# Attention K/V prefix projections moved between the steps of the gated linear attention stage

## The chip, the cores and the metric

The kernel runs on all eight cores of one Trainium2 chip, the same program on each. The time is the device time of the slowest core in microseconds. Nothing is exchanged between the cores. PE is TensorE (PEld its weight loads), DVE VectorE, ACT ScalarE, POOL GpSimd, SP SyncE.

## The reference, cut to what matters

One layer of a decoder for two groups of requests: two new prompts of 4096 tokens, and 32 sequences that each get 4 new tokens.

```
h = rmsnorm(x);  proj = h @ w_in        # gq gk gv gg glr | aq ak av
log_a = log_sigmoid(glr @ w_gk_up + b_gk) / 16
gla:  S_t = diag(a_t) S_{t-1} + k_t^T v_t ;  o_t = q_t S_t        (4 heads, 128 x 256 state)
att:  each query sees keys t - j*dil, j = 0..128, for dil 1, 4, 16  (8 heads of 128)
x = x + concat(rmsnorm(gla_o) * silu(gg), rmsnorm(att_o)) @ w_out
y = rmsnorm(x + square(relu(rmsnorm(x) @ w_up)) @ w_down)
```

D_MODEL is 2048. A core owns 1024 prompt tokens and the 16 new tokens of four sequences. To have the GLA state and the keys of up to 2048 earlier tokens, it computes these for the tokens before its own as well.

## The kernel before

A core goes through its prompt in four groups of 1024 tokens, `for g in range(4)`; group 3 holds its own tokens, groups 0 to 2 the prefix. For each group:

1. **Norm** (`ssq_norm`). SP and POOL by turns load 16 chunks of x into four buffers; ACT squares, DVE scales into `hT`, PE sums the squares with a matrix of ones, and DVE and POOL multiply by the inverse root. `hT` is bf16, 16 chunks of 128 features.
2. **GLA** (`gla_group`, L648). PE projects the low-rank gate, then K and V of head 0. Then for each of the 4 heads 14 steps are issued (in a prefix group): A1 for each half of 512 tokens (gate matmuls, then ACT), A2 for each half (cumulated gate, ACT, DVE at L587, POOL's multiply at L589), A3 for each half (transposes, ACT), and 8 state steps B, one for 128 tokens. B is a PE matmul, then DVE's update of the state `Sf` (L641), then POOL's cast to `Sb` (L644). Behind each step comes one item of the next head's projections (`proj_items`, L659): 2 K items of 16 matmuls 128x512, then 8 V tiles of 16 matmuls 128x256. Head 3 has no next head, and its steps follow one another bare.
3. **K/V prefix** (`kv_prefix_group`, L781), in groups 1 and 2 only, between two barriers. For each of the 8 attention heads, K and V are projected for the group's 1024 tokens: 4 items of 16 matmuls 128x512, each copied by ACT to a staging buffer of `kvst`, and stored by SP to a scratch tensor in HBM, which attention reads much later.

After group 3 come the K/V outputs, the attention heads, the attention of the 16 new tokens, w_out, and the MLP; none of this changes.

**Order and waits.** Each engine executes its own instructions in program order. `P.op` collects for each operation the operations it depends on, through trackers (`Trk`) of what last wrote a tile and what has read it since. `emit` turns each dependency into a wait instruction of its own (L110), unless the engine has already waited for that value or a later one of the same semaphore. So an operation that overwrites a tile issues one wait for each of the matmuls that read it, except those that an earlier wait covers. A barrier makes every engine wait for the last operation of each engine and the last transfer of every DMA slot.

**Weights.** `w_in` lies in HBM in fp32 (`wflat`) and is cast to bf16 by the DMA, which POOL issues (L290). `wload` (L403) has the list of all loads in order, and when load i is asked for it has issued load i + 1 as well; the blocks go round in three buffers (`wblk`):

```python
while len(wstate["issued"]) <= min(i + 1, len(WLIST) - 1):
    wstate["issued"].append(_wissue(WLIST[len(wstate["issued"])]))
```

A prefix head's block (128 columns of K, 128 of V) and a GLA head's V block are 1024 KB as written, a K block 512 KB. All matmuls are recorded at line 319 (transposes at 322), ACT's at 325. `AT` is a buffer of 16 chunks for the results of both attentions; groups 0 to 2 don't use it. `sqb` are two buffers of the norm stage, 1040 columns each.

Of the kernel before, what the change touches and what calls it, by code (L numbers as in the profile page):

```python
# [190 lines left out]
WLIST = None  # L191
# [32 lines left out]
def _build(nc, P):  # L224
# [64 lines left out]
    def dma(q, out, in_, reads=(), writes=()):  # L289
        return P.op(q, lambda e: e.dma_start(out=out, in_=in_), reads=reads, writes=writes, dma=True)  # L290
# [36 lines left out]
    class Rot:  # L327
        def __init__(self, arena, shape, dt, n):
            self.b = [arena.alloc(shape, dt) for _ in range(n)]
            self.t = [Trk() for _ in range(n)]  # L330
            self.i = 0

        def get(self):
            k = self.i % len(self.b)
            self.i += 1
            return self.b[k], self.t[k]
# [66 lines left out]
    def wload(col_specs, src=None, rows=None):  # L403
        i = wstate["i"]
        wstate["i"] += 1
        if WLIST is None:
            WLOG.append(col_specs)
            return _wissue(col_specs)
        assert WLIST[i] == col_specs
        while len(wstate["issued"]) <= min(i + 1, len(WLIST) - 1):  # L410
            wstate["issued"].append(_wissue(WLIST[len(wstate["issued"])]))
        return wstate["issued"][i]

    def proj_fm(wb, wt, wc, m, parts, evac):
        for (c0, n) in parts:
            ps, pt = ps_f()
            for kc in range(16):
                mm(ps[0:m, 0:n], wb[:, kc, wc:wc + m], hT[:, kc, c0:c0 + n], kc == 0, kc == 15,
                   reads=[wt, hT_t[kc]], writes=[pt])
            evac(ps, pt, c0, n)  # L420
# [224 lines left out]
            return stageB  # L645
        return [A1, A2, A3], [mk(i) for i in range(4)]

    def gla_group(g, own):  # L648
        parts = PARTS_OWN if own else PARTS_PRE
        N = NTOK if own else 1024  # L650
        P.op("pool", lambda e: e.memset(glrT[:, 0:N], 1.0), writes=[glrT_t])
        wb, wt = wload([(0, C_GLR, 16)])

        def ev_glr(ps, pt, c0, n):
            act(glrT[0:16, c0:c0 + n], ps[0:16, 0:n], AF.Copy, reads=[pt], writes=[glrT_t])
        proj_fm(wb, wt, 0, 16, parts, ev_glr)
        ntile = 9 if own else 8

        def proj_items(h, G):  # L659
            gkT, gkT_t, gqT, gqT_t, gv, gv_t, ggs, ggs_t = (G["gkT"], G["gkT_t"], G["gqT"], G["gqT_t"], G["gv"], G["gv_t"],  # L660
                                                            G["ggs"], G["ggs_t"])
            cols = [(0, C_GK + h * 128, 128)] + ([(128, C_GQ + h * 128, 128)] if own else [])
            wb, wt = wload(cols)

            def ev_k(ps, pt, c0, n):
                act(gkT[:, c0:c0 + n], ps[:, 0:n], AF.Copy, reads=[pt], writes=[gkT_t])

            def ev_q(ps, pt, c0, n):
                P.op("dve", lambda e: e.tensor_copy(out=gqT[:, c0:c0 + n], in_=ps[:, 0:n]), reads=[pt], writes=[gqT_t])
            for p_ in parts:  # L670
                proj_fm(wb, wt, 0, 128, [p_], ev_k)
                yield
            if own:
                for p_ in parts:
                    proj_fm(wb, wt, 128, 128, [p_], ev_q)
                    yield
            wb, wt = wload([(0, C_GV + h * 256, 256)])
            for ti in range(ntile):
                m = 128 if ti < 8 else 16

                def ev_v(ps, pt, ti=ti, m=m):
                    P.op("dve", lambda e: e.tensor_copy(out=gv[0:m, ti, :], in_=ps[0:m, 0:256]), reads=[pt], writes=[gv_t[ti]])  # L682
                proj_tm(wb, wt, 256, ti * 128, m, ev_v)
                yield
            if own:
                wb, wt = wload([(0, C_GG + h * 256, 256)])
                for vh in range(2):
                    def ev_g(ps, pt, c0, n, vh=vh):
                        act(ggs[:, vh, c0:c0 + n], ps[:, 0:n], AF.Silu, reads=[pt], writes=[ggs_t])
                    for p_ in parts:  # L690
                        proj_fm(wb, wt, vh * 128, 128, [p_], ev_g)
                        yield

        def head_norm(h, G):
            ggs, ggs_t = G["ggs"], G["ggs_t"]
            pss = [ps_f() for _ in parts]
            for vh in range(2):
                q, qt = sqb.get()
                act(q[:, 0:N], o_h[:, vh, 0:N], AF.Square, reads=[o_t], writes=[qt])
                for (c0, n), (ps, pt) in zip(parts, pss):  # L700
                    mm(ps[:, 0:n], onesb[:], q[:, c0:c0 + n], vh == 0, vh == 1, reads=[qt, ct], writes=[pt])
            for (c0, n), (ps, pt) in zip(parts, pss):
                act(sgate[:, c0:c0 + n], ps[:, 0:n], AF.Ln, reads=[pt, ct], writes=[sgate_t], scale=1.0 / 256,
                    bias=epsb[:, 0:1])
            act(sgate[:, 0:N], sgate[:, 0:N], AF.Exp, reads=[sgate_t], writes=[sgate_t], scale=-0.5)
            for vh in range(2):
                P.op("dve", lambda e, vh=vh: e.scalar_tensor_tensor(
                    out=o_h[:, vh, 0:N], in0=o_h[:, vh, 0:N], scalar=nw[:, NW_GLA + vh:NW_GLA + vh + 1],
                    in1=sgate[:, 0:N], op0=ALU.mult, op1=ALU.mult), reads=[o_t, sgate_t, ct], writes=[o_t])
                P.op("pool", lambda e, vh=vh: e.tensor_mul(out=AT[:, 2 * h + vh, 0:N], in0=o_h[:, vh, 0:N],  # L710
                                                          in1=ggs[:, vh, 0:N]),
                     reads=[o_t, ggs_t], writes=[AT_t[2 * h + vh]])

        for _ in proj_items(0, GB[0]):
            pass
        for h in range(4):
            G = GB[h % 2]
            nxt = proj_items(h + 1, GB[(h + 1) % 2]) if h < 3 else None
            (a0, b0), (a1, b1) = gla_batch(h, 0, own, G), gla_batch(h, 1, own, G)
            steps = [a0[0], a1[0], a0[1], a1[1], a0[2], a1[2]] + b0 + b1  # L720
            if own:
                steps.append(lambda h=h, G=G: gla_tile(h, 1024, 16, own, True, G))
                steps.append(lambda h=h, G=G: head_norm(h, G))
            nit = (24 if own else 10)
            per = -(-nit // len(steps))
            for st in steps:
                st()
                if nxt is not None:
                    for _ in range(per):
                        if next(nxt, "done") == "done":  # L730
                            nxt = None
                            break
            if nxt is not None:
                for _ in nxt:
                    pass

    A3 = Arena(nc, A1_mark)
    ks_s = A3.alloc([16, 1024], F32)
# [39 lines left out]
    atts_b = A3.alloc([16, 1024], BF16)  # L778
    atts_bt = Trk()

    def kv_prefix_group(g):  # L781
        for h in range(8):
            wb, wt = wload([(0, C_AK + h * 128, 128), (128, C_AV + h * 128, 128)])
            for which in range(2):
                st_, stt = kvst.get()

                def ev(ps, pt, c0, n, st_=st_, stt=stt):
                    act(st_[:, c0:c0 + n], ps[:, 0:n], AF.Copy, reads=[pt], writes=[stt])
                proj_fm(wb, wt, which * 128, 128, PARTS_PRE, ev)
                dma("sp", kvscr[which, h, :, (g - 1) * 1024:g * 1024], st_[:], reads=[stt], writes=[kvscr_t[which][h]])  # L790

    def kv_outputs():
        for which, (cb, outd, outs, sdst, sdt) in enumerate(((C_AK, k_o, ks_o, ks_s, ks_t), (C_AV, v_o, vs_o, vs_s, vs_t))):
# [216 lines left out]
    for g in range(4):  # L1010
        own = g == 3
        if DEBUG == "gla0" and not own:
            continue
        parts = PARTS_OWN if own else PARTS_PRE

        def src_chunks(kc, g=g, own=own):
            b, t = xc.get()
            dma("sp" if kc % 2 == 0 else "pool", b[:, 0:1024], xTv[kc, :, g * 1024:(g + 1) * 1024], writes=[t])
            if own:
                P.op("pool", lambda e, b=b, kc=kc: e.tensor_copy(out=b[:, 1024:1040], in_=xs_all[:, kc, :]), reads=[xs_t], writes=[t])  # L1020
            return b[:, 0:(NTOK if own else 1024)], [t]
        ssq_norm(src_chunks, parts, NW_ATTN, hT, hT_t, 2048.0)
        dumpf(0, rB[:, :], [rB_t])
        dumpb(0, hT[:, 0, :], [hT_t[0]])
        dumpb(1, hT[:, 15, :], [hT_t[15]])
        gla_group(g, own)
        if g in (1, 2):
            P.barrier()
            kv_prefix_group(g)
            P.barrier()  # L1030
    for h in range(4):
        dma("sp", gst_o[h], Sf[:, h, :], reads=[Sf_t[h]])
    P.barrier()
# [256 lines left out]
```

How the kernel before makes its waits and increments, by code:

```python
            def run(ename, eng):  # L98
                waited = {}
                for o in ops:
                    if o.eng != ename:
                        continue
                    for d in sorted(o.deps):
                        do = ops[d]
                        if do.dma:
                            sem, key = dsem[do.eng][do.slot], ("d", do.eng, do.slot)
                        else:
                            sem, key = csem[do.eng], ("c", do.eng)
                        if waited.get(key, 0) < do.val:
                            eng.wait_ge(sem, do.val)
                            waited[key] = do.val
                    if o.fn is None:
                        continue
                    ins = o.fn(eng)
                    if o.dma:
                        ins.then_inc(dsem[ename][o.slot], 16)
                    elif o.inc:
                        ins.then_inc(csem[ename], 1)
```

## Time and profile before

| | |
|---|---|
| median of the runs shown | 3796.25 us (3791.42 and 3801.07) |
| the profiled execution | 3794.15 us, span of its slowest core 3792.6 us |
| spans of the eight cores | 3767.1 to 3792.6 us |
| mean granted TensorE clock | 0.80 to 0.81 on every core |
| PE busy | 2777.2 us (73%) |
| DVE, ACT, POOL busy | 1197.2, 818.6, 813.4 us |
| chain that ended last | PE 63%, DMA 15%, issue 6%, ACT 6%, DVE 6%, POOL 4% |
| norm, group 1 | about 232 to 306 us |
| GLA, group 1 | 306.3 to 445.2 us |
| K/V prefix, group 1 | 445.2 to 557.4 us |
| norm, GLA, prefix of group 2 | to 630, 769 and 881.5 us |
| MLP | 2712 to 3690 us |

Times are from the first instruction of the slowest core, core 1. "Granted clock" is the share of full speed that TensorE was given: 1.00 is 2.4 GHz, 0.50 is 1.2 GHz. A timeline row is a run of like instructions: its start, the time from the first to the last, the engine and line, what it writes and reads, the count, and in brackets how long the engine was idle before it and what ended that. Waits and DMA issues themselves are not counted as busy time.

### The profile page before, as it was taken

The page shows a single profiled execution, that of the slowest core. Times are in us where ns is not written, and L with a number is a line of the kernel's source. Part 1 is how long each engine was busy: PE and PEld are TensorE (multiplying, and loading weights), DVE is VectorE, ACT ScalarE, POOL GpSimd, SP SyncE. Part 2 cuts the span into 40 slices and gives each one's busy share as a digit, 9 for nine tenths or more (in the row PEclk, how much of TensorE's full clock was granted, in tenths as well). Part 3 has the DMA queues.
Part 4 walks back from the last instruction along what each step waited for, and adds up shares of the span by engine and source line. Part 5 has one row for each costly group of instructions (what it writes and reads, how often), then busy time and mean ns, then how long its engine had stood idle before and what let it go on. Part 6 is the DMA issues. An engine that isn't in the chain of part 4 may idle for free.

```text
span 3792.6 us, 65066 instructions; the slowest of 8 cores (3767.1 to 3792.6 us)
## 1 busy us (share of the span) xinstructions
PE 2777.2 (73%) x17044; PEld 1474.5 (39%) x17044; DVE 1197.2 (32%) x2009; ACT 818.6 (22%) x2051; POOL 813.4 (21%) x1293
## 2 busy tenths in 40 slices
PE   2857886894888588767777222358499999999995
PEld 0635533641454375333333100023144444444443
DVE  3232203202222202333334433341343434243434
ACT  2131112112123212443344222220200010101003
POOL 3122103201221202222223233420311121211110
PEclk9968897996888598666666555568799999999998
DMA  4232343253332243112110144454234334342422
GB/s 116 45 90 51 70 106 98 45 109 109 57 63 50 67 111 74 29 40 45 29 29 18 17 70 69 72 106 112 45 57 79 66 69 76 59 87 49 90 46 91
DMA packets 76667, 257.02 MB, mean 68 GB/s; under 512 B 11609, under 2 KB 25433, under 8 KB 64898
## 3 DMA queue, kind: packets, MB, share of 16 engines
q0 software_dynamic: 43136, 186.93, 26.6%
q1 hardware_dynamic: 33170, 65.92, 5.0%
q8 instruction: 148, 2.42, 0.2%
q14 instruction: 213, 1.74, 0.1%
HBM read 394.89 MB, written 28.05 MB: 112 GB/s over the span
## 4 chain that ended last, share of the span: by engine, by line
PE 63%; DMA 15%; issue 6%; ACT 6%; DVE 6%; POOL 4%; ACTq 0%; POOLq 0%; DVEq 0%; SPq 0%
PE psf L319 60%; ACT sb L325 6%; DMA sb<-wflat 4%; DMA sb<-xT 3%; PE psb L322 3%; DMA sb<-ck 2%; DMA sb<-cv 2%; DVE sb L376 2%; POOL sb L376 1%; DMA sb<-wo_flat 1%; DVE sb L933 1%; DVE sb L929 1%; POOL sb L1110 1%; DVE sb L641 1%; DVE sb L1144 0%
## 5 line engine op out<-in xcount | busy, mean ns | idle before, releaser
L319 PE MATMUL psf<-sb,sb 128*128 128x512 bf16 (+8 forms) x16316 | 2717.3, 318 | 933.5 <-ACT sb L325 342.0
L319 PEld LDWEIGHTS psf<-sb,sb 128*128 128x128 bf16 (+3 forms) x16316 | 1413.0, 105 | 2179.9 <-issue 1262.6
L325 ACT ACTIVATE sb<-psf 128x512 f32<-128x512 f32 (+7 forms) x585 | 264.2, 465 | 1956.9 <-PE psf L319 1792.0
L1118 DVE TENSOR_TENSOR sb<-sb,psf 128x512 f32<-128x512 f32 (+1 forms) x768 | 380.9, 516 | 624.4 <-PE psf L319 613.1
L325 ACT ACTIVATE sb<-sb 128x1024 bf16<-128x1024 f32 (+7 forms) x273 | 185.4, 696 | 571.2 <-DVE sb L936 239.3
L857 DVE TENSOR_TENSOR sb<-sb,psf 128x128 f32<-128x128 f32 (+2 forms) x424 | 217.3, 512 | 264.3 <-PE psf L319 194.1
L848 POOL TENSOR_TENSOR sb<-sb,sb 128x64 bf16<-128x64 f32 (+3 forms) x424 | 164.6, 402 | 407.8 <-ACT sb L325 404.9
L1110 POOL TENSOR_TENSOR sb<-sb 128x512 bf16<-128x512 f32 (+1 forms) x192 | 146.5, 763 | 459.0 <-ACT sb L325 445.6
L325 ACT ACTIVATE sb<-psb 64x128 bf16<-64x128 bf16 (+4 forms) x488 | 140.4, 296 | 282.7 <-PE psb L322 249.3
L322 PE MATMUL psb<-sb,sb 128*128 128x128 bf16 (+3 forms) x584 | 155.4, 301 | 48.2 <-POOL sb L589 30.2
L366 DVE TENSOR_SCALAR sb<-sb,sb 128x1024 bf16<-128x1024 f32 (+1 forms) x80 | 57.6, 757 | 358.0 <-DMA sb<-xT 200.2
L325 ACT ACTIVATE sb<-psf,sb 128x64 f32<-128x64 f32 (+5 forms) x463 | 148.6, 370 | 9.7 <-PE psf L319 7.2
L682 DVE CAST sb<-psf 128x256 bf16<-128x256 f32 x132 | 56.0, 424 | 263.1 <-PE psf L319 243.3
L376 POOL TENSOR_TENSOR sb<-sb,sb 128x1024 bf16<-128x1024 bf16 (+1 forms) x40 | 124.1, 3134 | 68.8 <-ACT sb L325 68.8
L290 POOL DMA_DIRECT2D sb<-wflat x80 | 44.6, 559 | 396.6 <-PE psf L319 372.8
L929 DVE TENSOR_TENSOR sb<-sb,psf 128x512 f32<-128x512 bf16 x96 | 65.8, 685 | 199.6 <-PE psf L319 164.0
L376 DVE TENSOR_TENSOR sb<-sb,sb 128x1024 bf16<-128x1024 bf16 (+1 forms) x40 | 114.3, 2927 | 24.9 <-ACT sb L325 24.9
L322 PEld LDWEIGHTS psb<-sb,sb 128*128 128x128 bf16 (+3 forms) x584 | 78.6, 141 | 96.2 <-issue 70.3
L644 POOL CAST sb<-sb 128x256 bf16<-128x256 f32 x128 | 51.6, 403 | 237.6 <-DVE sb L641 181.4
L820 DVE CAST sb<-psf 128x512 bf16<-128x512 f32 (+1 forms) x24 | 12.5, 519 | 284.6 <-PE psf L319 284.5
L641 DVE SCALAR_TENSOR_TENSOR sb<-sb,sb,psf 128x256 f32<-128x256 f32 x128 | 61.0, 477 | 105.1 <-PE psf L319 87.6
L325 ACT ACTIVATE sb<-sb,sb 128x128 bf16<-128x128 bf16 (+1 forms) x194 | 78.9, 407 | 26.8 <-DMA sb<-v_s 6.4
(63 smaller groups left out, 597.0 us busy)
## 6 DMA issues: line engine op xcount, KB each, us to landing
sb<-wflat POOLq DMA_DIRECT2D x56, 1024.0 KB, 9.2
sb<-wu_flat POOLq DMA_DIRECT2D x16, 2048.0 KB, 15.4
sb<-w_down POOLq DMA_DIRECT2D x16, 2048.0 KB, 13.9
sb<-xT SPq DMA_DIRECT2D x48, 512.0 KB, 5.4
sb<-xT POOLq DMA_DIRECT2D x32, 512.0 KB, 6.0
sb<-wflat POOLq DMA_DIRECT2D x20, 512.0 KB, 5.0
kvscr<-sb SPq DMA_DIRECT2D x32, 256.0 KB, 3.1
sb<-kvscr SPq DMA_DIRECT2D x16, 512.0 KB, 5.0
```

The costliest lines, as they stand in the source:

```text
L319: P.op("pe", lambda e: e.matmul(out, lhsT=lhsT, rhs=rhs, start=start, stop=stop), reads=reads, writes=writes)
L322: P.op("pe", lambda e: e.transpose(out, in_, ident), reads=reads, writes=writes)
L325: P.op("act", lambda e: e.activation(out=out, in_=in_, func=func, **kw), reads=reads, writes=writes)
L366: P.op("dve", lambda e, kc=kc, s_ap=s_ap: e.tensor_scalar_mul(out=dst[:, kc, 0:N], in0=s_ap, scalar1=nw[:, nw_col + kc:nw_col + kc + 1]), ...
L376: P.op(eng, lambda e, kc=kc: e.tensor_mul(out=dst[:, kc, 0:N], in0=dst[:, kc, 0:N], in1=rB[:, 0:N]), reads=[dst_t[kc], rB_t], writes=[dst_ ...
L641: P.op("dve", lambda e: e.scalar_tensor_tensor(out=Sf[:, h, :], in0=Sf[:, h, :], scalar=bl[:, i:i + 1], in1=psS[:, 0:256], op0=ALU.mult, o ...
L682: P.op("dve", lambda e: e.tensor_copy(out=gv[0:m, ti, :], in_=ps[0:m, 0:256]), reads=[pt], writes=[gv_t[ti]])
L848: P.op("pool", lambda e, p_=p_, e_=e_, nk=nk, nq=nq, mbase=mbase: e.tensor_mul(out=p_[0:nk, 0:nq], in0=e_[0:nk, 0:nq], in1=amask[0:nk, mba ...
L857: P.op("dve", lambda e, ps2=ps2, qsl=qsl, nq=nq: e.tensor_add(out=acc[:, :, qsl], in0=acc[:, :, qsl], in1=ps2[:, 0:512].rearrange("p (a b) ...
L929: P.op("dve", lambda e, pr=pr, Kb=Kb, hh=hh: e.tensor_mul(out=pr[:, hh * 512:(hh + 1) * 512], in0=Kb[:, hh * 512:(hh + 1) * 512], in1=psQ[ ...
L1110: P.op("pool", lambda e, hb=hb, r_=r_, fc=fc, c0=c0, n=n: e.tensor_mul(out=hb[:, fc, c0:c0 + n], in0=r_[:, 0:n], in1=r_[:, 0:n]), reads=[r ...
L1118: P.op("dve", lambda e, ps=ps, dc=dc, c0=c0, n=n: e.tensor_add(out=x1T[:, dc, c0:c0 + n], in0=x1T[:, dc, c0:c0 + n], in1=ps[:, 0:n]), read ...
```

## The change

The prefix projections become a generator, `kv_prefix_items(g)`, which yields after each item of 16 matmuls, 32 items in all. `gla_group` takes it as `extra` and draws one item after each step, behind the item of the next head's projections; what is left at the end is drawn then. The two barriers around the prefix stage are gone. The weights no longer come through `wload`: the generator issues the load of a head's block itself, from POOL, into one half of the chunks 0 to 7 of `AT`, by turns, and goes on with that head's first item. The outputs are staged in the two buffers of `sqb`.

```diff
--- before.py
+++ after.py
@@ -645,7 +645,7 @@
             return stageB
         return [A1, A2, A3], [mk(i) for i in range(4)]
 
-    def gla_group(g, own):
+    def gla_group(g, own, extra=None):
         parts = PARTS_OWN if own else PARTS_PRE
         N = NTOK if own else 1024
         P.op("pool", lambda e: e.memset(glrT[:, 0:N], 1.0), writes=[glrT_t])
@@ -730,9 +730,14 @@
                         if next(nxt, "done") == "done":
                             nxt = None
                             break
+                if extra is not None and next(extra, "done") == "done":
+                    extra = None
             if nxt is not None:
                 for _ in nxt:
                     pass
+        if extra is not None:
+            for _ in extra:
+                pass
 
     A3 = Arena(nc, A1_mark)
     ks_s = A3.alloc([16, 1024], F32)
@@ -778,16 +783,40 @@
     atts_b = A3.alloc([16, 1024], BF16)
     atts_bt = Trk()
 
-    def kv_prefix_group(g):
+    class _Alias:
+        def __init__(self, rot):
+            self.rot, self.i = rot, 0
+
+        def get(self):
+            k = self.i % len(self.rot.b)
+            self.i += 1
+            return self.rot.b[k], self.rot.t[k]
+    kvst2 = _Alias(sqb)
+
+    def kv_prefix_items(g):
         for h in range(8):
-            wb, wt = wload([(0, C_AK + h * 128, 128), (128, C_AV + h * 128, 128)])
+            kvw_flat = AT[:, 4 * (h % 2):4 * (h % 2) + 4, :].rearrange("p a b -> p (a b)")[:, 0:4096]
+            kvw_t = AT_t[4 * (h % 2):4 * (h % 2) + 4]
+            key = ((C_AK + h * 128, 128), (C_AV + h * 128, 128))
+            if WLIST is None:
+                WOFF.setdefault(key, None)
+                dma("pool", kvw_flat[:, 0:16], wflat[:, 0:16], writes=kvw_t)
+            else:
+                dma("pool", kvw_flat, wflat[:, WOFF[key]:WOFF[key] + 4096], writes=kvw_t)
+            wb = kvw_flat.rearrange("p (kc n) -> p kc n", kc=16)
             for which in range(2):
-                st_, stt = kvst.get()
+                st_, stt = kvst2.get()
 
                 def ev(ps, pt, c0, n, st_=st_, stt=stt):
                     act(st_[:, c0:c0 + n], ps[:, 0:n], AF.Copy, reads=[pt], writes=[stt])
-                proj_fm(wb, wt, which * 128, 128, PARTS_PRE, ev)
-                dma("sp", kvscr[which, h, :, (g - 1) * 1024:g * 1024], st_[:], reads=[stt], writes=[kvscr_t[which][h]])
+                for (c0, n) in PARTS_PRE:
+                    ps, pt = ps_f()
+                    for kc in range(16):
+                        mm(ps[:, 0:n], wb[:, kc, which * 128:(which + 1) * 128], hT[:, kc, c0:c0 + n], kc == 0, kc == 15,
+                           reads=list(kvw_t) + [hT_t[kc]], writes=[pt])
+                    ev(ps, pt, c0, n)
+                    yield
+                dma("sp", kvscr[which, h, :, (g - 1) * 1024:g * 1024], st_[:, 0:1024], reads=[stt], writes=[kvscr_t[which][h]])
 
     def kv_outputs():
         for which, (cb, outd, outs, sdst, sdt) in enumerate(((C_AK, k_o, ks_o, ks_s, ks_t), (C_AV, v_o, vs_o, vs_s, vs_t))):
@@ -1023,11 +1052,7 @@
         dumpf(0, rB[:, :], [rB_t])
         dumpb(0, hT[:, 0, :], [hT_t[0]])
         dumpb(1, hT[:, 15, :], [hT_t[15]])
-        gla_group(g, own)
-        if g in (1, 2):
-            P.barrier()
-            kv_prefix_group(g)
-            P.barrier()
+        gla_group(g, own, kv_prefix_items(g) if g in (1, 2) else None)
     for h in range(4):
         dma("sp", gst_o[h], Sf[:, h, :], reads=[Sf_t[h]])
     P.barrier()
```

## Rows read from the trace of the kernel before

**Rows 1.** Busy time by stretch; its first line names the columns

```profile
core 1: us, PE busy (x) PEld busy (x) DVE busy (x) ACT busy (x) POOL busy (x), PEclk, DMA share, GB/s
...
306.30:445.20 138.90, 113.64 (x833) 86.45 (x833) 33.43 (x72) 24.61 (x48) 24.56 (x46) 0.90 0.25 49
...
445.20:557.40 112.20, 112.19 (x512) 50.35 (x512) 0.00 (x0) 18.54 (x31) 4.29 (x8) 0.99 0.48 102
...
425.00:445.00 20.00, 9.02 (x54) 6.93 (x51) 7.80 (x15) 4.87 (x10) 6.82 (x14) 0.66 0.00 1
...
445.20:448.30 3.10, 3.10 (x8) 1.14 (x9) 0.00 (x0) 0.00 (x0) 1.12 (x2) 0.50 0.00 0
...
448.30:455.00 6.70, 6.70 (x33) 3.01 (x31) 0.00 (x0) 1.20 (x2) 0.00 (x0) 1.00 0.87 147
```

**Rows 2.** PE's waits, GLA stage, then prefix stage: total us, times, longest

```profile
PE psf L319 <- DMA sb<-wflat: 10.8, 3, 4.2
...
PE psb L322 <- POOL sb L589: 8.4, 3, 5.7
...
PE psf L319 <- POOL sb L644: 7.3, 1, 7.3
```

**Rows 3.** The chain of waits that ended last: start us, us, what

```profile
238.99 5.02 DMA sb<-xT
...
299.30 6.87 DMA sb<-wflat
...
368.01 7.37 DMA sb<-wflat
...
400.13 7.58 DMA sb<-wflat
...
445.20 112.21 PE psf L319 x512
...
558.17 2.03 DMA kvscr<-sb
...
560.76 6.63 DMA sb<-xT
...
623.05 6.86 DMA sb<-wflat
```

**Rows 4.** Timeline, first GLA stage, up to the first A1 steps

```profile
313.92 0.53 POOL L290 DMA_DIRECT2D sb<-wflat  x1 [8.96 <-PE psf L319]
...
327.28 4.22 PEld L319 LDWEIGHTS psf<-sb,sb 17*128 17x128 f32 x24 [0.21 <-issue]
...
331.92 9.71 PEld L319 LDWEIGHTS psf<-sb,sb 17*128 17x128 f32 x72 [0.42 <-issue]
```

**Rows 5.** Timeline of heads 0 to 2 in the same stage

```profile
337.62 0.67 ACT L325 ACTIVATE sb<-psf 128x512 f32<-128x512 f32 x2 [0.29 <-PE psf L319]
...
339.17 1.03 POOL L589 TENSOR_TENSOR sb<-sb,sb 128x512 bf16<-128x512 f32 x1 [24.72 <-DVE sb L587]
...
347.74 0.59 POOL L290 DMA_DIRECT2D sb<-wflat  x1 [7.53 <-issue]
...
349.55 0.58 PE L322 MATMUL psb<-sb,sb 128*128 128x128 bf16 x4 [5.66 <-POOL sb L589]
...
364.64 0.48 DVE L641 SCALAR_TENSOR_TENSOR sb<-sb,sb,psf 128x256 f32<-128x256 f32 x1 [0.70 <-PE psf L319]
...
365.25 0.40 POOL L644 CAST sb<-sb 128x256 bf16<-128x256 f32 x1 [0.78 <-DVE sb L641]
...
368.01 0.59 POOL L290 DMA_DIRECT2D sb<-wflat  x1 [2.35 <-PE psf L319]
...
381.76 1.91 PE L319 MATMUL psf<-sb,sb 128*128 128x256 bf16 x16
```

**Rows 6.** POOL's queue, wait instructions of line 110 in 340 to 348 us

```profile
L110 POOLq EVENT_SEMAPHORE  x117: 17/17/17, 340.0 to 347.8; - x117
```

**Rows 7.** DMA issues in 440 to 560 us: count, KB each, median us to landing

```profile
sb<-wflat POOLq DMA_DIRECT2D x7, 1024.0 KB, 9.8
```

## The prediction

> **What bounds the kernel now.** I read the stages first, then what the matmul engine waits for in them, then the weight loads' place on the chain of waits and on POOL's stream. Groups 1 and 2 of the prompt each run one GLA stage and one K/V prefix stage; the second group repeats the first, so I work on group 1 and count twice. Its GLA stage is 138.9 us with PE busy for 113.6; the prefix stage is 112.2 us with PE busy for 112.2 [rows 1]. So only the GLA stage has holes: about 25 us. Of these, 5.7 is a wait for POOL and 4.2 twice a wait for a weight load (the third of the three, 2.4, is head 0's and stays) [rows 2]; 11 lie in the last 20 us, the fourth head, which has no projections to put between its steps [rows 1]. The prefix stage is sheer matmul work, 3.5 us for each of 32 items of 16 matmuls [rows 1, 3]. Its loads take 9.8 us [rows 7] and cost nothing, since each is asked for a whole head (14 us) ahead.
>
> **What changes, part by part.** (1) The 32 prefix items are put one behind each of the first 32 of 56 GLA steps, that is in heads 0 and 1 and four steps of head 2. PE's work is the same. The fourth head, with the 11 us of holes, gets none: no gain there. (2) The prefix weights no longer come through the prefetching loader. The generator asks POOL for head j's block and then emits, in the same turn, the first matmuls that read it. There are two buffers, but nothing is asked for early. Load j sits at step 4j, behind all that POOL has to do up to there. (3) The barriers go.
>
> Price of a load. Alone in flight in a GLA stage, a block of this size takes 7.4 to 7.6 us from issue to landing [rows 3]; in the prefix stage, with other traffic, the median is 9.8 [rows 7]. I take 7.5, since the new ones are mostly alone, and keep 9.8 for the range. The Trainium skill, "DMA: Bandwidth & Descriptors", section on the anatomy of a software-queue DMA, gives 2.0 us plus the bytes at 436 GB/s, so 4.4 us for 1 MiB; by that each stall below would be 3.1 us shorter and the sum +72 us instead of +115. The rows measured this very transfer, so they decide.
>
> Price of the waits ahead of it. Before a load may overwrite a buffer, POOL executes one wait for every matmul that read it: 117 are recorded in the 7.5 us hole before one issue [rows 5, 6], and a buffer with 32 readers has a hole of 2.35 us [rows 5]. That is 60 to 73 ns a wait. A prefix block has 64 readers: 3.8 to 4.7 us, I take 4.1. It is due where block j-2 was read after POOL's last wait, in both groups from j=2 on.
>
> Price of what gates POOL. In a state step (B) PE's matmul releases DVE's 0.48 us and that POOL's cast; with hand-overs the cast starts 0.75 us after the matmul, and the waits begin with it [rows 5]. In an A2 step ACT, DVE and POOL take 2.7 us from the matmul to the end of POOL's multiply [rows 5].
>
> Now each load j, timed from the matmul that gates it; PE's own work before it needs the block is a V tile of 1.9 us [rows 5], a K item of 3.5, a prefix item of 3.5, the gate matmuls of an A1 or A2 step 1.1 (two A1 steps start 4.6 us apart with a K item between [rows 4]), transposes 0.6.
> - j=0, step 0: nothing gates it but the load before it, issued at 313.9; PE comes to it only after the first A1 (327.3) and a K item, at 332 [rows 4]. Two loads of 7.5 in a row land by 329: no stall.
> - j=1, step 4: from the first A2 matmul POOL has 2.7, then a load with 128 waits (7.5), the second multiply (1.1), so the issue is at 12.0 and the landing at 19.5, up to 21.5 as the other transfer is still under way. PE arrives at 14.4. Stall 5.1 to 7.1, taken 6.1.
> - j=2 and j=5, B steps with a V tile: 0.75 + 4.1 + 7.5 - 1.9 = 10.4 each.
> - j=3 and j=6, B steps at which the projections of the next head have run out, so nothing lies between: 12.3 each.
> - j=4, A2 step: POOL's multiply starts at 1.7, then a K load with some 32 waits, then this one with some 48: issue at 6.8, landing 14.3 to 16.4, PE there at 1.9. Stall 12.3 to 14.5, taken 13.
> - j=7, step 28: issue at 5.2 behind another load, landing 12.7 to 16.2; PE has 3.5 + 1.1 + 3.5 to do. Stall 4.6 to 8.1, taken 6.3.
> Sum 70.8 us a group.
>
> What goes: the three stalls of 5.7, 4.2 and 4.2 [rows 2], since those loads and multiplies now have two items more of PE's work, or one of the new stalls, in front: -14.1.
>
> The clock: PE's granted clock is 0.50, the 1.2 GHz level, in the 3.1 us after PE restarts from a hole of 7 us, and 1.00 behind it [rows 1]. Each restart so loses 1.6 us of matmul work. Seven new ones, three fewer old ones: +6.2. The prefix items, which now run dense at the full level, are the ones that pay.
>
> The barrier behind the prefix stage: its last matmul ends at 557.4; the barrier drains the last store, and the first x load of POOL goes out at 560.8 [rows 3], the next group's weight load at 623.1, 65.7 us in all. Between groups 0 and 1, where there is no barrier, it is 60.3 us from that x load (239.0) to the weight load (299.3) [rows 3]: -5.3. It includes two x chunks that SP then loads early. The barrier ahead of the prefix stage makes PE wait 7.3 us for the last cast [rows 2], but without it the next norm stage stands behind the same chain of DVE and POOL: 0, between -7.3 and 0.
>
> Edits at nothing: the store of an item from two staging buffers instead of three (a store lands in 2.0 us [rows 3], a buffer comes round after two times two steps); 32 more copies on ACT, which is mostly idle in the stage [rows 1]. Were they all on the path, +19 us a group (0.6 each), which the range needn't hold.
>
> Sum for a group: 70.8 - 14.1 + 6.2 - 5.3 = +57.6 us, for both +115. The profiled execution took 3794.2 us (span 3792.6), 2.1 below the median of the runs shown; 3796.3 + 115 = **3911 us**, slower by 3.0%.
>
> **Bounds.** Low: shortest waits and loads (66 of stalls), the whole 7.3 of the first barrier back: +46 a group, 3888. With the loads at 9.8 us: +16 a group and the upper ends of j=1, 4, 7 (+4): 3952.
>
> **Rivals.**
> A, not slower: POOL gets to the loads early. The mechanism is j=0's: where no operation of POOL hangs on a recent matmul, the issue runs ahead of PE. If that held at all eight, the change would give -14.1 - 4.7 - 5.3 = -24.1 a group, 3748 us. The point that decides: the average stall, its restart at half clock included, must stay under 3.4 us (24.1 over 7). For it: the load at 313.9 is issued 18 us before use [rows 4]. Against it: at four of seven places the operation just before is the cast of the same step, and a 1 MB load never lands under 7.4 us; the ordinary loads, asked for a step or two ahead, still stall PE by 4.2 us [rows 2]. Chance 0.05; even this ends within 2%. Partly hidden stalls (about half, 3800 to 3870): 0.09.
> B, longer loads: seven of eight take the 9.8 us of the prefix stage, because of stores and other loads in flight: 3944. For it: [rows 7]; against: in the GLA stage only two loads per head compete. Chance 0.18.
> C, the interleaving pays more than I see, through the barriers and the fourth head: all holes of PE gone gives at most 25 + 7 a group, 3732 us. Against it: the items run out at step 32. Chance 0.02.
> D, the ACT and DVE chains are late behind the prefix copies: up to +19 a group on top, 3949. It needs ACT behind PE, while ACT is busy for 24.6 of 138.9 us [rows 1]. Chance 0.04.
> The forecast itself: 0.62.
>
> **Numbers.** About 2% (76 us, so 3872) is what a measurement can tell from no change. Slower: the forecast, B, D and a little of the partly hidden case, 0.86. Same: A and most of the partly hidden, 0.12. Faster 0.02. Range: 3862 to 3962.
>
> **What would show it.** In the changed kernel's trace PE should wait seven times in each of the two groups for the prefix weights' load, 5 to 14 us each, about 71 us in sum; on POOL some 64 waits should stand before each such issue; the three old stalls of the stage should be gone; the granted clock should drop after each hole; the stage from the first K item to the last cast should last some 314 us instead of 139 + 112; the fourth head should still take 20 us. Wrong would be: few or short waits for that load (A), or loads of 10 us (B). If PE's new waits are on ACT or DVE, D.

## The result, and the profile after

The changed kernel takes **3933 us** (median of 12 runs) against 3799 us for the kernel before (10 runs beside them): ratio **1.036**, 95% interval 1.034 to 1.039, slower by 134 us. Forecast were 3911 us and a range of 3862 to 3962. Some executions of every kernel, the one before too, fall into a slower condition of the chip that hits one die; ratios here come from undisturbed runs alone, and a time in microseconds behind a ratio is that ratio times 3799 where the median is disturbed.

The profiled execution's slowest core is core 0, with a span of 3927.8 us. First, where the time went. These are lines of the chain of waits of the changed kernel (start, us, what): the weight load that ends the norm stage of groups 2 and 3 (group 1's, at 301.66, stands among POOL's rows below).

```profile
698.19 6.58 DMA sb<-wflat
...
1102.51 10.14 DMA sb<-wflat
```

And the same one of the kernel before for group 3; those of groups 1 and 2 stand in [rows 3].

```profile
966.45 9.92 DMA sb<-wflat
```

Timeline rows of POOL after: the issue of group 1's weight load, the last cast of its GLA stage, the first x load of the next norm stage, and the last cast of group 2.

```profile
301.66 1.14 POOL L290 DMA_DIRECT2D sb<-wflat  x2
...
636.90 0.79 POOL L644 CAST sb<-sb 128x256 bf16<-128x256 f32 x1 [0.78 <-DVE sb L641]
637.64 1.12 POOL L290 DMA_DIRECT2D sb<-xT  x2
...
1029.65 0.40 POOL L644 CAST sb<-sb 128x256 bf16<-128x256 f32 x1 [0.78 <-DVE sb L641]
```

From the weight load of one group to that of the next it was 323.8 and 343.4 us (299.3, 623.05, 966.45) and is now 396.5 and 404.3 us (301.7, 698.2, 1102.5): +72.8 and +60.9, together 133.7 of the 134 us. These are the two slowest cores, core 1 before and core 0 after; the medians of all eight cores agree (324.2 and 341.8 us before, 395.6 and 405.6 after, together +135.2). So outside groups 1 and 2 next to nothing moved. Within them, GLA and prefix took 258.1 and 258.5 us before (299.3 to 557.4, 623.05 to 881.5) and take 336.0 and 331.9 now, up to the last cast: +77.9 and +73.4. From there to the next weight load it took 65.7 and 85.0 us and takes 60.6 and 72.5: -5.1 and -12.5.

What PE waits for in the interleaved stage of group 1, from the waits view (total us, times, longest); the rows that answer to [rows 2]:

```profile
PE psf L319 <- DMA sb<-wflat: 84.5, 7, 14.8
PE psb L322 <- POOL sb L589: 3.0, 2, 1.6
```

Seven waits for a weight load (310 to 640 us, so without head 0's own), where there were two in the run of the steps, and the one for POOL's multiply is gone. In group 2 they are seven again, 82.2 us. The timeline of PE shows each of the seven; the idle time before the row and what ended it stand in brackets.

```profile
369.20 5.93 PE L319 MATMUL psf<-sb,sb 128*128 128x512 bf16 x16 [9.33 <-DMA sb<-wflat]
...
404.53 17.88 PE L319 MATMUL psf<-sb,sb 128*128 128x512 bf16 x83 [11.50 <-DMA sb<-wflat]
436.21 27.06 PE L319 MATMUL psf<-sb,sb 128*128 128x512 bf16 x134 [13.80 <-DMA sb<-wflat]
478.03 12.21 PE L319 MATMUL psf<-sb,sb 128*128 128x512 bf16 x55 [14.75 <-DMA sb<-wflat]
...
514.45 21.03 PE L319 MATMUL psf<-sb,sb 128*128 128x512 bf16 x114 [11.51 <-DMA sb<-wflat]
549.45 21.58 PE L319 MATMUL psf<-sb,sb 128*128 128x512 bf16 x89 [13.97 <-DMA sb<-wflat]
580.70 26.27 PE L319 MATMUL psf<-sb,sb 128*128 128x512 bf16 x134 [9.66 <-DMA sb<-wflat]
```

All seven rows begin with a 128x512 matmul, a prefix item; they are j=1 to 7, and j=0 has no stall. Now POOL, ahead of the second of them: its issue rows in the timeline, the wait instructions in 390 to 397 us, and the loads in the chain with issue and time to landing.

```profile
396.69 0.53 POOL L290 DMA_DIRECT2D sb<-wflat  x1 [4.29 <-issue]
...
427.53 0.53 POOL L290 DMA_DIRECT2D sb<-wflat  x1 [4.00 <-issue]
```

```profile
L110 POOLq EVENT_SEMAPHORE  x67: 17/17/17, 391.9 to 396.7; - x67
```

```profile
358.42 10.64 DMA sb<-wflat
396.69 7.70 DMA sb<-wflat
427.53 8.16 DMA sb<-wflat
469.43 8.46 DMA sb<-wflat
506.61 7.70 DMA sb<-wflat
540.61 8.71 DMA sb<-wflat
568.85 11.71 DMA sb<-wflat
```

For 4.8 us POOL does nothing but get through 67 waits (the profile names no operation that it waited for), and only then does it issue a load that takes 7.7 us. And the clock, in two stretches (columns as in [rows 1]) behind the first stall, and over the stage:

```profile
308.70:642.90 334.20, 232.26 (x1325) 135.66 (x1344) 35.31 (x74) 44.13 (x82) 30.14 (x56) 0.84 0.29 63
...
369.20:372.30 3.10, 3.10 (x8) 1.14 (x9) 0.00 (x0) 0.00 (x0) 0.00 (x0) 0.50 0.00 0
372.30:376.00 3.70, 3.70 (x22) 1.92 (x20) 0.00 (x0) 0.78 (x2) 0.00 (x0) 0.78 0.00 0
```

In the first 3.1 us the granted clock is 0.50, the 1.2 GHz level, and eight matmuls of 512 columns get through instead of the fourteen of the dense stage before (512 in 112.2 us, at 0.99).

### The profile page after: what moved, and what is told of

It is laid out like the page before. It is cut to its first block, busy times and chain, and to the rows that moved or that the text cites. A ratio compares the mean times of both kernels' runs of the same rounds, so it can differ in the third digit from the quotient of the medians.

```text
span 3927.8 us, 64107 instructions; the slowest of 8 cores (3906.4 to 3927.8 us)
## 1 busy us (share of the span) xinstructions
PE 2771.7 (71%) x16816; PEld 1474.6 (38%) x17044; DVE 1196.8 (30%) x2009; ACT 815.1 (21%) x2051; POOL 814.5 (21%) x1293
## 4 chain that ended last, share of the span: by engine, by line
PE 60%; DMA 17%; issue 7%; DVE 6%; ACT 6%; POOL 4%; POOLq 0%; ACTq 0%; DVEq 0%; another core or an unknown queue 0%; SPq 0%
PE psf L319 58%; DMA sb<-wflat 6%; ACT sb L325 5%; DMA sb<-xT 3%; DMA sb<-ck 3%; PE psb L322 2%; DMA sb<-cv 2%; DVE sb L376 2%; POOL sb L376 1%; DMA sb<-wo_flat 1%; DVE sb L962 1%; POOL sb L1135 1%; DVE sb L641 1%; DVE sb L1143 1%; POOLq L110 0%
## 5 line engine op out<-in xcount | busy, mean ns | idle before, releaser
L319 PE MATMUL psf<-sb,sb 128*128 128x512 bf16 (+12 forms) x16088 | 2711.4, 318 | 1088.6 <-ACT sb L325 338.9
L319 PEld LDWEIGHTS psf<-sb,sb 128*128 128x128 bf16 (+4 forms) x16316 | 1412.9, 105 | 2326.5 <-issue 1429.4
L325 ACT ACTIVATE sb<-psf 128x512 f32<-128x512 f32 (+8 forms) x585 | 263.6, 464 | 2115.5 <-PE psf L319 1877.6
L849 DVE CAST sb<-psf 128x512 bf16<-128x512 f32 (+1 forms) x24 | 12.5, 520 | 283.7 <-PE psf L319 283.5
L589 POOL TENSOR_TENSOR sb<-sb,sb 128x512 bf16<-128x512 f32 x32 | 36.2, 1130 | 300.9 <-DVE sb L587 298.3
L587 DVE TENSOR_TENSOR sb<-sb,sb 128x512 f32<-128x512 f32 x32 | 23.7, 740 | 241.8 <-ACT sb L325 238.7
## 6 DMA issues: line engine op xcount, KB each, us to landing
sb<-wu_flat POOLq DMA_DIRECT2D x16, 2048.0 KB, 13.7
```

Source lines behind the costliest of these rows:

```text
L319: P.op("pe", lambda e: e.matmul(out, lhsT=lhsT, rhs=rhs, start=start, stop=stop), reads=reads, writes=writes)
L325: P.op("act", lambda e: e.activation(out=out, in_=in_, func=func, **kw), reads=reads, writes=writes)
```

## The experiments

Two theories were set against each other. **L**: the loss is the prefix loads, each asked for at its first use, with 64 waits ahead of it. **I**: cutting the dense prefix stage up costs by itself (copies, clock, order). Ratios are to the kernel before, with 95% intervals.

**e1_prefetch: the loads one head ahead.**

```diff
+        blocks = [load(0)]
         for h in range(8):
-            (load of head h, as in the change)
+            if h < 7:
+                blocks.append(load(h + 1))
+            wb, kvw_t = blocks[h]
```

> The changed kernel, but the prefix weights are asked for one head ahead: the blocks of heads 0 and 1 at the first step, and that of head h + 1 when head h's items begin, into the same two buffers. Theory L (the loss is late loads): PE's waits for the prefix weights, 84 us in group 1 of the changed kernel, go to under 5 us a group, and what is left is the gain that the prediction gave its rival A, 14.1 + 4.7 + 5.3 = 24 us a group: 3751 us, ratio to the kernel before 0.987. Theory I (the interleaving itself costs: copies on ACT, the dense stage cut up, the clock): the waits go but the time stays above the kernel before, 3810 to 3870. Theory Q (POOL's queue has no room, so even an early load is issued late): stalls of 5 us and more stay at most of the heads, above 3850.

Measured: 0.984 (0.983 to 0.986), about 3740 us. PE's waits in 299 to 720 us, which hold all of group 1's steps and the norm stage behind them:

```profile
PE psf L319 <- DMA sb<-wflat: 2.1, 2, 1.1
```

The 84.5 us of waits have become 2.1, and the kernel is 5% faster than the changed one, 1.6% faster than the one before. Theory I and the expectation's Q (POOL's queue has no room for an early load) fall: everything else of the change is still in, and it pays. From one group's first K item to the next one's it is 296.8 and 316.9 us on core 1 against 323.7 and 346.5 before: -27 and -29.5 a group, where the prediction's rival A had put -24.1.

**e2_onewait: no string of waits ahead of the loads.** Only the first and last matmul of a prefix head carry the block's trackers.

```diff
-reads=list(kvw_t) + [hT_t[kc]]
+reads=(list(kvw_t) if (which, c0, kc) in ((0, 0, 0), (1, 512, 15)) else []) + [hT_t[kc]]
```

> The changed kernel, but only the first and the last matmul of a prefix head are booked as readers of its weight block (PE works in order, so the last stands for all), which leaves 2 waits instead of 64 ahead of a load; position and size of the loads are the same. Theory L with the waits on the path: six of the seven stalled loads are issued 2.9 to 4.2 us sooner, about 23 us a group, so 3933 - 47 = 3886 us, ratio 1.023; the hole of 4.0 to 4.3 us on POOL before those issues goes to under 0.3. If the waits were hidden behind something else (the queue's descriptor work, or the cast), no change: 3933, ratio 1.035.

Measured: 1.026 (1.024 to 1.027), 3896 us: -37 us (-40 by the ratios), where 47 were expected. POOL's hole is gone, here ahead of the load for head 2, and PE's stall behind it is 7.3 us instead of 11.5 (two rows of two timelines):

```profile
391.62 0.53 POOL L290 DMA_DIRECT2D sb<-wflat  x1 [0.24 <-PE psf L319]
```

```profile
399.30 18.42 PE L319 MATMUL psf<-sb,sb 128*128 128x512 bf16 x84 [7.29 <-DMA sb<-wflat]
```

The waits are on the path at their full length at such a place; the sum over seven, 63.9 us instead of 84.5, falls somewhat less than I put. The first stall stays (9.8 us, 9.3 before), and those of j=4 and j=7 fall by only 1.6 and 1.5 us: their loads now go out right behind another one, 0.6 us later, and take 9.7 and 14.3 us, longer than with the waits in between.

**e3_nobarrier: the kernel before without the two barriers.**

```diff
-            P.barrier()
             kv_prefix_group(g)
-            P.barrier()
 ...
-                st_, stt = kvst.get()
+                st_, stt = sqb.get()
```

> The kernel before, with its prefix stage in one piece behind the GLA stage and its prefetching loader, but without the two barriers around it, and with the two norm buffers for staging (so that nothing overlaps in memory). The prediction's term for the barriers: -5.3 us a group behind the stage and 0 ahead of it, 3788 us, ratio 0.997. Rival C (the barriers cost more than their edges, as the first wait of 7.3 us is taken back too): -12.6 a group, 3774 us, ratio 0.993. Barriers free: 3799.

Measured: 0.9995 (0.9966 to 1.0023). The -11 us of the prediction lie inside the interval, and so does nothing at all; -25 do not. The profile says -5.9 and -7.9 us for the two groups (K item to K item on core 1, 317.9 and 338.5 us). The time alone leaves the term open; with the profile, it is small. It also comes from the other edge than I had put. PE now starts the prefix stage 0.8 us after its last state matmul, where it had waited 7.3 us for the last cast [rows 2] (a row of PE, core 5):

```profile
439.10 112.76 PE L319 MATMUL psf<-sb,sb 128*128 128x512 bf16 x512 [0.81 <-DVE sb L641]
```

Behind the prefix stage little is gained: on core 5 it is 63.9 us from its last matmul to the next weight load, against 66.0 on the same core before. So with the stage in one piece it is the barrier ahead of it that costs, and the -5.3 us behind it is not what this run shows.

**e4_warm: PE kept busy through the stalls.**

```diff
+            if h > 0:
+                ps, pt = ps_f()
+                for _ in range((0, 40, 50, 60, 64, 50, 60, 40)[h]):
+                    mm(ps[:, 0:512], onesb[:], hT[:, 0, 0:512], True, True, reads=[ct, hT_t[0]], writes=[pt])
```

> The changed kernel, but PE multiplies a matrix of ones with a chunk of the activations into an unused result bank while it would wait for a prefix block: 40 to 64 matmuls of 512 columns for each head from 1 on, 8.6 to 13.8 us at full clock, each a little less than the stall measured there. It tells the clock term from the waiting. Theory L with the prediction's clock term (1.6 us lost at each restart): the granted clock stays at 1.00 over the seven places and 11 us a group come back, 3933 - 22 = 3911 us, ratio 1.030. If the clock costs nothing beyond the wait (the prefix item behind it is not on the path), 3933, ratio 1.035; if the extra matmuls run over their holes, up to 3945.

Measured: 1.030 (1.028 to 1.032): by the ratios -25 us against the changed kernel, uncertain by some 11 us, 22 expected. The loads get no shorter (10.8 and 7.4 us for j=1 and 2, against 10.6 and 7.7); what changes is the item behind it, 3.6 us here instead of the 5.9 of the first row above, and the granted clock over the stage, 0.95 instead of 0.84:

```profile
370.81 3.61 PE L319 MATMUL psf<-sb,sb 128*128 128x512 bf16 x16 [0.80 <-DMA sb<-wflat]
```

```profile
310.00:640.00 330.00, 305.20 (x1719) 170.15 (x1720) 38.90 (x79) 49.43 (x87) 31.60 (x58) 0.95 0.31 68
```

Useless matmuls made the kernel faster. So some 25 us of the loss are clock, not waiting. The Trainium skill ("TensorE: Matmul & The Clock Gate", section "HAM oscillation — how this bites in real kernels") describes a matmul kernel whose bursts are shorter than its waits for a transfer; PE falls back to its low clock in each wait, so that every burst starts cold. The trace of the changed kernel agrees: the granted clock is 0.50 to 0.59 in the first 3.1 us behind each of its seven stalls. Its bursts aren't short, though: 18 to 27 us from one stall to the next.

**e8_split: the block as two loads, K first** (edit shortened)**.**

```diff
-dma("pool", kvw_flat, wflat[:, WOFF[key]:WOFF[key] + 4096], writes=kvw_t)
+for which in range(2):   # own key, own two chunks of AT, own trackers
+    dma("pool", flat, wflat[:, WOFF[key]:WOFF[key] + 2048], writes=tk)
```

> The changed kernel, still without an early load, but each prefix block comes as two loads of half the size, K's first, each with 32 waits ahead of it, into its own chunks; V's lands while K's items run. Theory L, with waits and transfer both on the path: a stall gets shorter by 2.1 us of waits and by about 2.5 us of transfer (a block of 512 KB takes 4.9 to 5.0 us in the profile before, one of 1024 KB 7.5), at seven places in two groups some 60 us: 3933 - 60 = 3873 us, ratio 1.020. If a load's time were all fixed cost, only the waits: 3933 - 28 = 3905, ratio 1.028.

Measured: 1.021 (1.019 to 1.022), 3879 us: -54 us (-59 by the ratios), 60 expected, and well clear of the 28 that the waits alone would give. So both the length of the transfer and the waits are on the path.

**e5, e6, e10: one wait per semaphore for each operation**, put into `emit` in place of one for each dependency; e5 is the kernel before with it, e6 is e1_prefetch, e10 is the changed kernel.

```diff
-                        if waited.get(key, 0) < do.val:
-                            eng.wait_ge(sem, do.val)
-                            waited[key] = do.val
+                        if need.get(key, (0, None))[0] < do.val:
+                            need[key] = (do.val, sem)
+                    for key, (val, sem) in need.items():
+                        if waited.get(key, 0) < val:
+                            eng.wait_ge(sem, val)
+                            waited[key] = val
```

> The kernel before, with one wait per semaphore for each operation (the highest value that any of its dependencies needs) in place of one for each dependency; nothing is moved. If the strings of waits on POOL are on the path as the prediction has it, the hole of 5.7 us on PE behind the load with 128 waits goes in all four groups and the weight load that PE waits 4.2 us for comes 2.3 us sooner, twice a group: about 10 us a group, 3798 - 40 = 3758 us, ratio 0.990, more if attention gains as well. If these waits are hidden, 3798.

Measured: 0.984 (0.982 to 0.986), -62 us, more than the 40 expected. In the chain of e5 the weight loads of groups 2 and 3 stand at

```profile
606.28 6.56 DMA sb<-wflat
...
936.27 9.73 DMA sb<-wflat
```

and that of group 1 at 293.0, so groups 1 and 2 gain 10.5 and 13.4 us (313.3 and 330.0 us instead of 323.8 and 343.4), as I had put. What I had left out is most of the rest of the kernel: from group 3's weight load on, 26.8 us of the 57.0 between the two profiled spans, where I had allowed 10. Some 16 of them lie between the first cache load of the new tokens' attention and the MLP's first weight load (569.8 and 553.3 us, medians of the eight cores).

> The changed kernel with the prefix weights asked for one head ahead, and one wait per semaphore for each operation. Ratio so far with the first alone: 0.984 (3739 us). In groups 1 and 2 PE now waits for hardly any load, so the strings of waits cost nothing there; in groups 0 and 3 they go as in the kernel before with single waits: 3739 - 20 = 3719 us, ratio 0.979. If groups 1 and 2 gain as well, down to 3700.

Measured: 0.975 (0.972 to 0.977), 3705 us, at the lower end of what was expected.

> The changed kernel as it stands, loads late, with one wait per semaphore for each operation; beside e5 (the kernel before with the same, ratio 0.9836) it tells what the change costs where waits cost nothing. Theory L: outside groups 1 and 2 it gains what e5 gains there (33 us), in them 18 us a group by the prefix loads' waits (measured in e2) and some 7 at the second load, behind the one with 128 waits: 3933 - 33 - 50 = 3850 us, ratio 1.0135, so still 3% behind e5. If the strings of waits were the whole loss, it would come out level with e5, at 0.984.

Measured: 1.011 (1.009 to 1.014), 3852 us. With all strings of waits gone the change still costs 2.8 points against e5, 105 us instead of 134. The strings make the loss larger; the greater part is the late loads themselves.

**e7, e9, e11: the fourth head filled.** The prediction had said that its holes stay because the items run out. On top of e6:

```diff
-                if extra is not None and next(extra, "done") == "done":
+                if extra is not None and not own and (h == 3 or si % 14 in SPREAD) and next(extra, "done") == "done":
 # SPREAD = (4, 10, 11, 12, 13, 2)
```

> As the last (prefix weights one head ahead, single waits), but the 32 prefix items go to all 14 steps of the fourth head and to six steps of each of the other three (2, 4 and 10 to 13) instead of to the first 32 steps. The prediction held that the 11 us of holes in the fourth head, and the half clock there, get nothing from the change: if they can be filled, PE's waits in the fourth head go and 14 us a group come back, 28 in all: 3691 us, ratio 0.972. If the chain of state updates through DVE and POOL, not PE, sets the fourth head's end, nothing: 3719. If heads 0 to 2 get holes for want of items, in between.

Measured: 0.978 (0.977 to 0.980), 3718 us, a miss: slower than e6 by 13 us. A new wait stands in PE's timeline:

```profile
340.63 8.87 PE L323 MATMUL psf<-sb,sb 128*128 128x512 bf16 x40 [13.40 <-DMA sb<-wflat]
```

The first block is asked for at step 2 now, and used at once. Twice this wait is 27 us of the 28 that were hoped for. So e9 asks for the first two blocks before head 0's projections.

> As e7_spread, but the first two prefix blocks are asked for before head 0's projections, as nothing there had to wait for them in the changed kernel. In e7_spread PE waited 13.4 us in each group for the first block, since its first item comes at step 2 and the load was asked for just before it. If that wait hid the gain of filling the fourth head: the two waits and their restarts go, 30 us, 3718 - 30 = 3688 us, ratio 0.970, faster than e6 (0.9745) by the fourth head's holes less what heads 0 to 2 lose. If the fourth head is set by the chain of DVE and POOL anyway, it comes out at e6's 3705.

Measured: 0.977 (0.976 to 0.979), 3720 us. The wait did not go, it changed its load: the row is now a 128x256 one, head 0's V block, which queues behind the two.

```profile
318.79 34.60 PE L323 MATMUL psf<-sb,sb 128*128 128x256 bf16 x240 [13.34 <-DMA sb<-wflat]
```

e11 moves the same request by three items:

```diff
-        if extra is not None:
-            next(extra)
-        for _ in proj_items(0, GB[0]):
-            pass
+        for n_, _ in enumerate(proj_items(0, GB[0])):
+            if n_ == 2 and extra is not None:
+                next(extra)
```

> As e9_primed, but the first two prefix blocks are asked for when head 0's first V tile has been issued, so behind the loads of head 0's K and V blocks and of head 1's K block on POOL. In e9_primed they stood ahead of head 0's V block, and PE waited 13.3 us for that one instead; in e7_spread it waited 13.4 us for the first prefix block. If this third place keeps both clear, the two waits and restarts go, 30 us: 3690 us, ratio 0.969. If a wait of that size turns up at yet another load (head 1's V block, now behind the two), 3720, ratio 0.977, as e7 and e9; e6 with 0.9745 would then be the best version.

Measured: **0.968** (0.960 to 0.975), about 3676 us by the ratio. The interval overlaps e6's, mostly for one run of the kernel before beside it, at 3836 us; e11's own three lie at 3677 to 3686 us, e6's at 3700 to 3707. The profiled run has a span of 3680.8 us on its slowest core, e6's 3705.1, and in 290 to 600 us PE waits 3.0 us for weight loads:

```profile
PE psf L323 <- DMA sb<-wflat: 3.0, 4, 1.7
```

The waits for POOL's multiply (L593 here), 2.9 us in e6's same window, are gone, and from one group's weight load to the next it is 287.2 and 305.3 us instead of e6's 297.9 and 310.3 (medians of the eight cores): 15.7 of the 28 us that e7 had put for the fourth head.

It is the fastest version found, 3.2% under the kernel before and 6.6% under the changed one.

## Why the prediction was right

Term by term, for group 1 and group 2:

| term | predicted | measured |
|---|---|---|
| stalls on prefix loads | +70.8 | +84.5, +82.2 |
| old stalls gone | -14.1 | -14 (two load waits and the multiply's are gone) |
| clock at the restarts | +6.2 net | e4 gets back 12 a group at the seven new ones, 10.9 had been put |
| GLA and prefix together | +62.9 | +77.9, +73.4 |
| norm stage behind it | -5.3 | -5.1, -12.5 |
| sum of both groups | +115 | +134 |

With the measured stalls in the sum, 84.5 - 14.1 + 6.2 = 76.6 and 74.3 us, the stage comes out within 1.3 us in both groups. That the total lies as near as 19 us is in part luck: the stalls were 25 us more than put for the two groups, and the norm stages gave back 7 us more than put.

- **The stalls' places** were right: none at j=0, then seven, in both groups. Their sizes: 9.3, 11.5, 13.8, 14.8, 11.5, 14.0 and 9.7 us against 6.1, 10.4, 12.3, 13.0, 10.4, 12.3 and 6.3.
- **The mis-sized term is the price of a load.** I took 7.5 us, from loads that were alone; these took 7.7 to 11.7, in the mean 9.0 (the seven chain rows above), two thirds of the way to the 9.8 of rival B. The two longest, 10.6 and 11.7, are j=1 and j=7, issued 1.6 and 4.7 us behind another load; I had named that for both, but had allowed only 1.0 and 1.7 us for what cost 3.1 and 4.2. The 1.5 us more in the mean make 10.6 us over the seven; less what the sum had allowed at j=1, 4 and 7 (3.3 in all), that is 7.3 of the 13.7 us of the difference. The waits are about 3 us more: from the start of the cast to the issue it was 4.7 us at j=2 and 5 and 4.4 at j=3 and 6, where 4.1 had been put, and at j=4 the issue came 6.3 us after the multiply's start instead of 5.1. The last 3 us are not taken apart.
- **The sentence from the Trainium skill's transfer formula** ("DMA: Bandwidth & Descriptors"; an estimate of 4.4 us for 1 MiB, which would have made the sum +72) was rightly set aside: no load of 1024 KB took under 7.4 us before or 7.3 after.
- **The waits ahead of a load** were on the path, as e2 and e8 show.
- **The barriers:** behind group 1 the -5.3 is met within 0.2. Behind group 2 it is 12.5, and the forecast had counted group 1's term twice. In group 3's norm stage POOL can issue its first x load only when SP's first chunk has landed. Before, SP's load stood behind the barrier, and POOL's went out 9.1 us after the last prefix matmul (881.5); after, SP's goes out at 1000.9, among the GLA steps, and POOL's at once behind the last cast. These are POOL's rows before and after:

```profile
890.57 0.71 POOL L290 DMA_DIRECT2D sb<-xT  x1 [0.28 <-issue]
```

```profile
1030.24 0.94 POOL L290 DMA_DIRECT2D sb<-xT  x1
```

  The barrier ahead of the prefix stage gave back nothing, in as far as the other terms leave no room for it; e3 shows that it does where the prefix stage follows in one piece.
- **The fourth head** got nothing from the change, as said: from its first multiply on POOL to the last cast's end it is 13.1 us before and after. e11 shows that it can gain, once all loads are early; e7 and e9 had lost that again at one late load.
- **Rival A** was wrong for the kernel as changed, and right as a mechanism: e1 makes its condition true, and comes out 59 us under the kernel before, where A had 48. **Rival B** is half true: the loads are longer, 9.0 us in the mean, but not seven of them take 9.8: five take 7.7 to 8.7, and only the two right behind another load take more. **C** and **D** did not show; PE has no wait on ACT over 0.7 us in the interleaved steps of group 1.

Not settled: why a load that is alone in flight takes 7.7 us at one place and 8.7 at another. Stores by SP and loads of the neighbouring cores are there in the profile, but nothing was run to part them.

## What to carry to other kernels

When work is moved into another stage to fill its holes, move its loads first, and then look at what each load now stands behind on its queue; a generator that asks for a block and uses it in the same turn has two buffers and no prefetch. Count the wait instructions that a dependency tracker puts ahead of an operation, above all on a queue that issues transfers. A stall on PE costs its length (9 to 15 us here) and then the slow restart (some 1.8 us each by e4).

## What the runs showed of the hardware

- A wait on POOL's queue that holds nothing up costs some 70 ns (67 in 4.8 us, 117 in 7.8 us). One wait per semaphore instead of one per dependency is worth 62 us (1.6%) on the kernel before, with no instruction moved.
- Matmuls with no use, put into PE's holes, made the kernel 25 us faster through the clock alone; 22 had been expected.
- Two transfers of 1024 KB asked for ahead of a third cost the third about 13 us of PE's time in e9, as much as asking for the first too late in e7: on one queue, a request has to be placed between too late and in the way.
